# The blocks of a triangular solve turned by small products with an identity in place of full transposes

## The chip, the core and the metric

The kernel runs on one core of a Trainium2 chip. The metric is the device time of one execution in microseconds (us). Lower is better.

## The reference

Two layers of a hybrid network over 1,024 tokens of width 1,024 are computed in float32. What matters here is the mixer of the first layer: its linear recurrence of eight heads of 64 channels, run once forward and once backward in time, whose two outputs are added.

```python
def step(state, inp):
    r_t, w_t, k_t, v_t, kk_t, a_t = inp
    sk = jnp.einsum('bhij,bhj->bhi', state, kk_t)
    state = (state * w_t[:, :, None, :]
             - sk[..., :, None] * (kk_t * a_t)[:, :, None, :]
             + v_t[..., :, None] * k_t[:, :, None, :])
    y = jnp.einsum('bhij,bhj->bhi', state, r_t)
    return state, y
```

The other parts are the attention of three dilations, the Fourier mixer, the gated convolutions and the norms. The change does not touch them.

## The kernel before

The recurrence is not run token by token. The 1,024 tokens are cut into 16 chunks of CH = 64, two chunks to a pair, so NPAIR = 8 pairs for each direction g (0 forward, 1 backward). The eight heads are KU = 4 pairs of heads f, each with two heads hh. Within a chunk the steps are tied together by a unit lower triangular matrix of 64x64 (built from `xn`), one for each head and each chunk c. There are 16 such matrices for each pair of chunks, and each has to be inverted.

The inverse is built in five levels (LEVELS 2, 4, 8, 16, 32) by doubling: blocks of size b that are already inverted are joined to blocks of size 2b. A level i has four steps, with the engine that does each:

- `turn_u` on TensorE: the present inverse (`X1` at level 0, `T` after it) is transposed into bank 2 of PSUM. ScalarE copies the result to `U` (L1915).
- `level_x` on TensorE (L1749): products of the triangular matrix with the present inverse. VectorE puts the wanted blocks into `XL` by a predicated copy (L2079).
- `level_t` on TensorE (L1780): products of `U` with `XL`. VectorE copies them to `T` (L2087, L2089). At the last level `last_u` (L1792) takes this place, and ScalarE copies its result to `T` (L1921).

`T` and `X1` hold 128 partitions by 8 matrices by 64 columns. The two chunks of a pair lie in the two halves of the partitions (`side(c)`), and the two heads of a pair lie in the two halves of the output's partitions after the turn (`head(hh)`). Each group g has four banks of PSUM of its own: `bank(g, 0)` to `bank(g, 3)`. Bank 2 takes the transposes. Bank 3 takes the products of `values` (L1732), which ScalarE copies to `rz` (L1909, semaphore `mv_c`), and in other steps parts of `turn`, `scores`, `solve`, `step_open` and `last_u`.

The order on each engine is written out by hand, in a loop of half steps h. In each half step one direction (a) goes through the five levels of its inverse, while the other (b) uses its finished inverse (`solve` L1804, `carry` L1815, `step_open` L1829 and L1834, `step_close` L1846 and L1850) and prepares its next pair (`turn` L1689, `scores` L1708, `lower` L1720, `values` L1732). In the next half step the two change places. Sixteen half steps have levels, so `turn_u` runs 80 times. TensorE's order within a half step is:

```
turn_u 0, level_x 0, solve, level_t 0, carry,
turn_u 1, level_x 1, step_open 1, level_t 1, step_open 0, step_close 0,
turn_u 2, level_x 2, step_close 1, level_t 2, turn (parts 0 and 1),
turn_u 3, level_x 3, scores 0, level_t 3, scores 1,
turn_u 4, level_x 4, lower, values, last_u
```

ScalarE's order is: the copy of `turn_u` 0, those of `solve`, the copies of `turn_u` 1 and 2 with other work between them, `tokens` part 0, `turn_u` 3, `tokens` part 1, exponentials, `turn_u` 4, `values`, `last_u`. SyncE loads five or six factors of 256 KB in each half step.

Most matrix products here are 64x64 pieces: they use one quadrant of TensorE's array, given by the half of the partitions that they read and the half that they write. The trace calls this form 64*64. A product in this form appears in the trace as two weight loads and two matmuls, as 16 calls give x32 in its rows. A full transpose (form 128*128) appears as one of each.

Of the kernel before, what the change touches and what calls it, by code (L numbers as in the profile page):

```python
# [11 lines left out]
ACT = mybir.ActivationFunctionType  # L12
AX = mybir.AxisListType

P = 128
# [522 lines left out]
CH = 64  # L538
# [3 lines left out]
KU = WA // P  # L542
# [934 lines left out]
def recurrence(nc, z_d, vr_d, lw_d, aa_d, kk_d, consts, ysum, mix_out, bon_d, gate_d, yb_d, factors, small):  # L1477
# [5 lines left out]
    ident = consts["ident"]  # L1483
# [3 lines left out]
    with ExitStack() as ctx:  # L1487
        s = Scope(nc, ctx, "rw")

        def both(name, shape, dt=F32):  # L1490
            return [s.sb(f"{name}{g}", shape, dt) for g in range(2)]
# [15 lines left out]
        X1, _, T, U = (both(n, [P, UN, CH]) for n in ("X1", "align", "T", "U"))  # L1507
# [12 lines left out]
        pb = s.ps("pb", [P, 8, 512])  # L1520
        pw = pb[:, :, :].rearrange("p k (f n) -> p (k f) n", n=P)

        def sems(name):
            return [s.sem(f"{name}{g}") for g in range(2)]
# [3 lines left out]
        turned, tok_c, q_done, q_c, l_done, x1_c, mv_done, mv_c = (sems(n) for n in (  # L1528
            "turned", "tok_c", "q_done", "q_c", "l_done", "x1_c", "mv_done", "mv_c"))
        x_done, x_c, t_done, t_c, u_done, u_c, z_done, z_c, rg_done, rg_c = (sems(n) for n in (  # L1530
            "x_done", "x_c", "t_done", "t_c", "u_done", "u_c", "z_done", "z_c", "rg_done", "rg_c"))
# [8 lines left out]
        def side(c):  # L1540
            return slice((1 - c) * CH, (2 - c) * CH)
# [4 lines left out]
        def head(hh):  # L1546
            return slice(hh * HD, (hh + 1) * HD)
# [10 lines left out]
        def bank(g, k):  # L1558
            return pb[:, 4 * g + k, :]
# [18 lines left out]
        def pair(f, hh):  # L1578
            return 2 * f + hh
# [86 lines left out]
        def _(pe):  # L1666
            mm = nc.tensor.matmul
# [84 lines left out]
            def turn_u(g, m, i):  # L1752
                if not 0 <= m < NPAIR:
                    return
                if i == 0:
                    pe.wait_ge(x1_c[g], 2 * m + 2)
                    pe.wait_ge(q_c[g], 4 * m + 3)
                else:
                    pe.wait_ge(t_c[g], (NL - 1) * m + i)
                src = X1[g] if i == 0 else T[g]  # L1760
                for f in range(KU):
                    ins = nc.tensor.transpose(bank(g, 2)[:, f * P:(f + 1) * P], src[:, 2 * f:2 * f + 2, :].rearrange("p h n -> p (h n)"),
                                              ident[:, :])
                ins.then_inc(u_done[g], 1)

            def level_t(g, m, i):
# [87 lines left out]
            for h in range(-1, 2 * NPAIR + 1):  # L1854
                a, p, b, q = h % 2, h // 2, 1 - h % 2, (h - 1) // 2
                turn_u(a, p, 0)
                level_x(a, p, 0)
                solve(b, q)
                level_t(a, p, 0)
                carry(b, q)  # L1860
                turn_u(a, p, 1)
                level_x(a, p, 1)
                step_open(b, q, 1)
                level_t(a, p, 1)
                step_open(b, q, 0)
                step_close(b, q, 0)
                turn_u(a, p, 2)
                level_x(a, p, 2)
                step_close(b, q, 1)
                level_t(a, p, 2)  # L1870
                turn(b, q + 1, 0)
                turn(b, q + 1, 1)
                turn_u(a, p, 3)
                level_x(a, p, 3)
                scores(b, q + 1, 0)
                level_t(a, p, 3)
                scores(b, q + 1, 1)
                turn_u(a, p, 4)
                level_x(a, p, 4)
                lower(b, q + 1)  # L1880
                values(b, q + 1)
                last_u(a, p)

        @block.scalar
        def _(act):
            A = nc.scalar.activation
# [24 lines left out]
            def turn_u(g, m, i):  # L1911
                if not 0 <= m < NPAIR:
                    return
                act.wait_ge(u_done[g], (NL + 1) * m + i + 1)
                A(U[g].rearrange("p (c f) n -> p f c n", c=2), bank(g, 2).rearrange("p (f c n) -> p f c n", c=2, n=CH), ACT.Copy).then_inc(u_c[g], 1)  # L1915

            def last_u(g, m):
                if not 0 <= m < NPAIR:
# [58 lines left out]
            for h in range(-1, 2 * NPAIR + 1):  # L1977
                a, p, b, q = h % 2, h // 2, 1 - h % 2, (h - 1) // 2
                turn_u(a, p, 0)
                solved_z(b, q)  # L1980
                solved_w(b, q)
                turn_u(a, p, 1)
                f_rates(a, p + 1)
                turn_u(a, p, 2)
                out(b, q, 0)
                out(b, q, 1)
                tokens(b, q + 1, 0)
                turn_u(a, p, 3)
                tokens(b, q + 1, 1)
                f_exp_in(a, p + 1)  # L1990
                f_exp_before(a, p + 1)
                turn_u(a, p, 4)
                f_exp_out(a, p + 1)
                values(b, q + 1)
                last_u(a, p)
# [1893 lines left out]
```

## Time and profile before

| what | value |
|---|---|
| median of 3 runs | 2735.75 us |
| lowest and highest of them | 2735.1 and 2738.48 us |
| span of the profiled execution | 2735.4 us |
| its time outside the span | no record of its own; 2735.4 stands for it |
| mean granted clock of TensorE | 0.963 |
| stretch of the recurrence | about 643 to 1012 us |

The profile is of one execution. The span goes from its first to its last instruction. A row of the timeline shows when a group began and how long it lasted in all; instructions in a group overlap, so that the distance from one start to the next is what a group costs its engine. PEld is the loading of weights, PE the matmul, DVE VectorE, ACT ScalarE, POOL GpSimd, SP SyncE. "Issue" in brackets is idle time that no semaphore of the profile ends. The queue called q8 carries the program's own instructions.

### The profile page before, as it was taken

What the parts mean: (1) busy time and instruction counts of PE and PEld (TensorE: products, weight loads), DVE (VectorE), ACT (ScalarE), POOL (GpSimd) and SP (SyncE); (2) the same over time, 40 slices, a digit from 0 to 9 for tenths busy, and PEclk for the clock granted to TensorE, in tenths of its full rate; (3) what the DMA queues carried; (4) which work ended last, traced back from release to release, by engine and by line L of the source; (5) the groups of instructions that cost most, each with busy time, mean ns of one, the idle gap of its engine ahead of it and who ended that gap; (6) DMA issues with size and microseconds to landing.
All of it is one profiled execution on the core that took longest, in us unless ns stands there. A gap on an engine that the chain in (4) does not pass through costs nothing. (4 is left out here: it accounts for less than half of the span.)

```text
span 2735.4 us, 51474 instructions
## 1 busy us (share of the span) xinstructions
PE 2545.9 (93%) x21459; PEld 2056.0 (75%) x21459; DVE 1554.7 (57%) x2258; ACT 1158.6 (42%) x1818; POOL 906.6 (33%) x629
## 2 busy tenths in 40 slices
PE   5998989898999989789999999996988999999998
PEld 4776656566888877678888888775767888888887
DVE  7775622464666646655555564456565555556445
ACT  5211252464555533434444444453443434444434
POOL 2301121212222202247877720001324787772000
PEclk7999999998999989999999999998999999999999
DMA  7686534812222123222323265441222232326554
GB/s 241 216 279 218 174 124 168 255 25 75 77 73 73 50 88 132 77 78 85 93 70 93 82 235 187 167 144 72 85 77 80 82 93 70 92 86 237 188 176 146
DMA packets 295914, 346.27 MB, mean 127 GB/s; under 512 B 28383, under 2 KB 224212, under 8 KB 295684
## 3 DMA queue, kind: packets, MB, share of 16 engines
q1 hardware_dynamic: 286044, 336.64, 37.7%
q10 hardware_dynamic: 9640, 6.33, 0.8%
q8 instruction: 172, 2.82, 0.4%
q14 instruction: 58, 0.48, 0.1%
HBM read 271.58 MB, written 71.34 MB: 125 GB/s over the span
## 5 line engine op out<-in xcount | busy, mean ns | idle before, releaser
L3138 POOL TENSOR_TENSOR cg_u_lo<-cg_u_raw,cg_u_hi 128x512 fp32r<-128x512 f32 x210 | 314.5, 1506 | 148.1 <-ACT cg_u_hi L3024 148.1
L131 PE MATMUL cg_ps<-m_hi,cg_u_hi 128*128 128x512 f32 x844 | 331.5, 393 | 26.1 <-DVE cg_u_lo L3213 21.8
L133 PE MATMUL cg_ps<-m_hi,cg_u_lo 128*128 128x512 f32 x844 | 330.8, 392 | 0.0
L132 PE MATMUL cg_ps<-m_lo,cg_u_hi 128*128 128x512 f32 x808 | 316.3, 391 | 0.0
L3024 ACT ACTIVATE cg_u_hi<-cg_u_raw 128x512 fp32r<-128x512 f32 x216 | 132.1, 629 | 381.0 <-PE cg_ps L133 230.6
L131 PEld LDWEIGHTS cg_ps<-m_hi,cg_u_hi 128*128 128x128 f32 x844 | 160.0, 190 | 61.2 <-DVE cg_u_lo L3213 22.6
L133 PE MATMUL cg_ps<-over_y_tx,cg_u_lo 128*128 128x512 f32 x480 | 186.9, 389 | 0.0
L132 PE MATMUL cg_ps<-over_y_tx,cg_u_hi 128*128 128x512 f32 x480 | 186.9, 389 | 0.0
L131 PE MATMUL cg_ps<-over_y_tx,cg_u_hi 128*128 128x512 f32 x480 | 186.9, 389 | 0.0
L133 PEld LDWEIGHTS cg_ps<-m_hi,cg_u_lo 128*128 128x128 f32 x844 | 159.9, 189 | 33.5
L3190 DVE SCALAR_TENSOR_TENSOR cg_z<-cg_ps,top_conv_f,cg_z 128x1023 f32<-128x1023 f32 x88 | 112.9, 1283 | 115.7 <-ACT cg_z L3048 115.7
L132 PEld LDWEIGHTS cg_ps<-m_lo,cg_u_hi 128*128 128x128 f32 x808 | 152.8, 189 | 31.6
L3138 POOL TENSOR_TENSOR cg_u_lo<-cg_u_s,cg_u_hi 128x512 fp32r<-128x512 f32 x80 | 103.6, 1296 | 63.7 <-ACT cg_u_hi L3024 63.7
L3193 DVE SCALAR_TENSOR_TENSOR cg_z<-cg_ps,top_conv_f,cg_z 128x1023 f32<-128x1023 f32 x88 | 112.9, 1283 | 3.1
L131 PE MATMUL za_ps<-h_hi,za_w_hi 128*128 128x512 f32 x256 | 105.8, 413 | 7.4 <-POOL za_w_lo L1039 7.4
L3048 ACT ACTIVATE cg_z<-cg_ps,top_conv_f 128x1024 f32<-128x1024 f32 x88 | 98.2, 1116 | 21.0 <-DVE cg_ps L3250 11.6
L132 PEld LDWEIGHTS cg_ps<-over_y_tx,cg_u_hi 128*128 128x128 f32 x480 | 90.1, 188 | 18.7
L133 PEld LDWEIGHTS cg_ps<-over_y_tx,cg_u_lo 128*128 128x128 f32 x480 | 90.1, 188 | 18.7
L131 PEld LDWEIGHTS cg_ps<-over_y_tx,cg_u_hi 128*128 128x128 f32 x480 | 90.1, 188 | 18.7
L131 PE MATMUL cg_ps<-over_f_d_hi,cg_a_hi 128*128 128x512 f32 x248 | 97.0, 391 | 6.4 <-DVE cg_a_lo L3209 6.4
L132 PE MATMUL za_ps<-h_lo,za_w_hi 128*128 128x512 f32 x256 | 102.8, 402 | 0.0
L133 PE MATMUL za_ps<-h_hi,za_w_lo 128*128 128x512 f32 x256 | 102.4, 400 | 0.0
(497 smaller groups left out, 6216.2 us busy)
## 6 DMA issues: line engine op xcount, KB each, us to landing
cg_u_raw<-in_ffn_up SPq DMA_DIRECT2D x88, 512.0 KB, 5.1
cg_u_raw<-in_ffn_down SPq DMA_DIRECT2D x64, 512.0 KB, 4.8
qkv_mw<-in_ada_w SPq DMA_DIRECT2D x12, 2048.0 KB
over_f_d_raw<-in_ffn_down SPq DMA_DIRECT2D x48, 512.0 KB, 5.0
scr_act<-cg_z SPq DMA_DIRECT2D x44, 512.0 KB, 2.7
qkv_mw<-in_ada_w SPq DMA_DIRECT2D x8, 1024.0 KB, 11.7
next_w<-in_mix_in SPq DMA_DIRECT2D x16, 512.0 KB, 6.0
za_out<-in_ada_w SPq DMA_DIRECT2D x8, 1024.0 KB
```

The costliest lines, as they stand in the source:

```text
L131: nc.tensor.matmul(out, a_hi, b_hi, start=first, stop=False)
L132: nc.tensor.matmul(out, a_hi, b_lo, start=False, stop=False)
L133: return nc.tensor.matmul(out, a_lo, b_hi, start=False, stop=last)
L3024: A(u_hi[:, n % RING], source(g, i), ACT.Copy).then_inc(uhi_done, 1)
L3048: A(z[:, x, :], both(g, x), ACT.Copy, scale=conv_cols[:, 1, g + x * FT:g + x * FT + 1]).then_inc(mid_done, 1)
L3138: G.tensor_tensor(u_lo[:, n % RING], source(g, i), u_hi[:, n % RING].bitcast(F32), ALU.subtract).then_inc(ulo_done, 1)
L3190: V.scalar_tensor_tensor(z[:, x, 1:S], both(g, x)[:, 0:S - 1], conv_cols[:, 0, c:c + 1], z[:, x, 1:S], ALU.mult, ALU.add).then_inc(left_do ...
L3193: V.scalar_tensor_tensor(z[:, x, 0:S - 1], both(g, x)[:, 1:S], conv_cols[:, 2, c:c + 1], z[:, x, 0:S - 1], ALU.mult, ALU.add).then_inc(con ...
```

## The change

At each of the 80 places the four full transposes of 128x128 are replaced by 16 products of 64x64: the piece of `X1` or `T` is the stationary operand, and the piece of the identity on the same partitions is the moving operand, so that the result is the piece transposed. The products for chunk c = 0 go to bank 3 and those for c = 1 to bank 2, in columns 0 to 255 of each. ScalarE's copy reads the two banks instead of one and writes `U` in its order in memory. As bank 3 is now written, the first `turn_u` of a half step waits for the copy of `values` out of it (`mv_c`), and for the fourth instead of the third masked copy of `scores` (`q_c`).

```diff
@@ turn_u on TensorE
                 if i == 0:
                     pe.wait_ge(x1_c[g], 2 * m + 2)
-                    pe.wait_ge(q_c[g], 4 * m + 3)
+                    pe.wait_ge(q_c[g], 4 * m + 4)
+                    pe.wait_ge(mv_c[g], m + 1)
                 else:
                     pe.wait_ge(t_c[g], (NL - 1) * m + i)
                 src = X1[g] if i == 0 else T[g]
                 for f in range(KU):
-                    ins = nc.tensor.transpose(bank(g, 2)[:, f * P:(f + 1) * P], src[:, 2 * f:2 * f + 2, :].rearrange("p h n -> p (h n)"),
-                                              ident[:, :])
+                    for hh in range(2):
+                        for c in range(2):
+                            ins = mm(bank(g, 3 - c)[head(hh), f * CH:(f + 1) * CH], src[side(c), pair(f, hh), :], ident[side(c), side(c)],
+                                     start=True, stop=True)
                 ins.then_inc(u_done[g], 1)
@@ turn_u on ScalarE
-                A(U[g].rearrange("p (c f) n -> p f c n", c=2), bank(g, 2).rearrange("p (f c n) -> p f c n", c=2, n=CH), ACT.Copy).then_inc(u_c[g], 1)
+                A(U[g].rearrange("p (c f) n -> p c (f n)", c=2), pb[:, 4 * g + 2:4 * g + 4, 0:KU * CH], ACT.Copy).then_inc(u_c[g], 1)
```

## Rows read from the trace of the kernel before

**Rows 1.** The page: span, busy times of TensorE, the instruction queue.
```profile
span 2735.4 us, 51474 instructions
...
PE 2545.9 (93%) x21459; PEld 2056.0 (75%) x21459; DVE 1554.7 (57%) x2258; ACT 1158.6 (42%) x1818; POOL 906.6 (33%) x629
...
q8 instruction: 172, 2.82, 0.4%
```

**Rows 2.** Busy times by window, inside the recurrence (from:to, length, engines, clock, DMA).
```profile
660.00:990.00 330.00, 320.21 (x9618) 289.72 (x9618) 196.07 (x408) 180.55 (x361) 69.19 (x55) 0.99 0.24 72
```

**Rows 3.** Groups by line and form, the recurrence: the transposes' matmuls.
```profile
L1762 PE MATMUL rw_pb<-top_ident,rw_T 128*128 128x128 f32 x256 | 41.8, 287 | 2.4 <-DVE rw_T L2089 1.6 <-DVE rw_T L2087 0.8
...
L1762 PE MATMUL rw_pb<-top_ident,rw_X 128*128 128x128 f32 x64 | 10.5, 287 | 0.0
```

**Rows 4.** Timeline of weight loads: four starts of the solve.
```profile
674.85 0.14 PEld L1804 LDWEIGHTS rw_pb<-rw_rz,rw_T 64*64 64x64 f32 x2
...
872.08 0.31 PEld L1804 LDWEIGHTS rw_pb<-rw_rz,rw_T 64*64 64x64 f32 x6
...
893.37 0.31 PEld L1804 LDWEIGHTS rw_pb<-rw_rz,rw_T 64*64 64x64 f32 x6
...
981.61 0.20 PEld L1804 LDWEIGHTS rw_pb<-rw_rz,rw_T 64*64 64x64 f32 x4
```

**Rows 5.** Timeline of weight loads between two gaps, 721 to 726 us.
```profile
721.00 0.21 PEld L1780 LDWEIGHTS rw_pb<-rw_XL,rw_U 64*64 64x64 f32 x8 [0.38 <-issue]
721.12 0.86 PEld L1815 LDWEIGHTS rw_pb<-rw_xn,rw_zt 64*64 64x64 f32 x32
722.16 0.42 PEld L1762 LDWEIGHTS rw_pb<-top_ident,rw_T 128*128 128x128 f32 x4 [0.18 <-DVE rw_T L2087]
722.75 0.56 PEld L1749 LDWEIGHTS rw_pb<-rw_T,rw_xn 64*64 64x64 f32 x32 [0.17 <-issue]
723.35 0.55 PEld L1829 LDWEIGHTS rw_pb<-rw_wv,rw_xn 128*64 128x64 f32 x16
723.81 0.55 PEld L1834 LDWEIGHTS rw_pb<-rw_xn,rw_wv 128*64 128x64 f32 x16
724.43 0.43 PEld L1780 LDWEIGHTS rw_pb<-rw_XL,rw_U 64*64 64x64 f32 x20
725.78 0.31 PEld L1780 LDWEIGHTS rw_pb<-rw_XL,rw_U 64*64 64x64 f32 x12 [0.92 <-issue]
```

**Rows 6.** DMA queues, windows 723.3:723.4, 834.2:834.3 and 837.5:837.7 us (packets, MB, share).
```profile
q8 instruction: 1, 0.02, 72.2%
...
q8 instruction: 1, 0.02, 55.5%
...
q8 instruction: 1, 0.02, 29.2%
```

**Rows 7.** Timeline of weight loads, 804 to 818 us.
```profile
804.31 0.56 PEld L1720 LDWEIGHTS rw_pb<-rw_st 64*64 64x64 f32 x32
804.78 1.03 PEld L1732 LDWEIGHTS rw_pb<-rw_wv,rw_xn 64*64 64x64 f32 x32
...
806.34 0.42 PEld L1762 LDWEIGHTS rw_pb<-top_ident,rw_X 128*128 128x128 f32 x4
...
807.39 1.51 PEld L1804 LDWEIGHTS rw_pb<-rw_rz,rw_T 64*64 64x64 f32 x28
...
815.05 0.54 PEld L1846 LDWEIGHTS rw_pb<-rw_es,rw_rg 64*64 64x64 f32 x16
815.51 0.55 PEld L1850 LDWEIGHTS rw_pb<-rw_rg,rw_es 64*64 64x64 f32 x16
816.13 0.43 PEld L1762 LDWEIGHTS rw_pb<-top_ident,rw_T 128*128 128x128 f32 x4
816.72 0.56 PEld L1749 LDWEIGHTS rw_pb<-rw_T,rw_xn 64*64 64x64 f32 x32 [0.16 <-issue]
817.19 0.55 PEld L1846 LDWEIGHTS rw_pb<-rw_es,rw_rg 64*64 64x64 f32 x16
```

**Rows 8.** Timeline of ScalarE: the copy of the values.
```profile
806.00 0.60 ACT L1909 ACTIVATE rw_rz<-rw_pb 128x512 f32<-128x512 f32 x1 [0.93 <-PE rw_pb L1732]
```

## The prediction

> **What bounds the kernel now.** I read the page first. TensorE is busy 93% of the span, and the queue that carries instructions has moved 172 packets [rows 1]. Then I looked at the recurrence by window: over 330 us TensorE is busy for 320 us at a clock of 0.99, while VectorE and ScalarE are busy for 196 and 181 us [rows 2]. So inside this stretch the order of TensorE is nearly closed, and what it costs from one start to the next sets the time. The recurrence stands between barriers, so its end moves the kernel's end one for one. The matmuls' mean of 287 ns [rows 3] can't be used for this: four of them begin within 0.43 us, because they overlap. The distances between starts have to be read from the timeline.
>
> A half step shows itself as the distance between two starts of the solve. From 674.85 to 981.61 us there are 14 of them, 21.91 us each. A half step in which nothing is late takes 893.37 - 872.08 = 21.29 us [rows 4]. So 0.62 us of each half step is lost to something that comes and goes. What it is matters most here.
>
> The rows between 721 and 726 us show it. Weight loads stop in the middle of a group at a gap called "issue", begin again at 721.00, stop again in the middle of a group, and begin again at 725.78, with 0.92 us idle before it. No semaphore ends either gap. Counted, there are 8 + 32 + 4 + 32 + 16 + 16 + 20 = 128 loads from the first gap to the second [rows 5]. Each load has its matmul, so 256 instructions. The page gives the same number from the other side: 42,918 loads and matmuls in 172 packets are 250 to a packet, and instructions that only wait, which these counts leave out, fill up the rest [rows 1]. A packet is thus 256 of TensorE's instructions, and a gap stands where one packet is used up and the next is not there. The packet for 725.78 is seen in the queue at 723.3 [rows 6], 2.4 us before its first use and 2.3 us after TensorE had begun the packet ahead of it. I read this as a supply one packet deep: the next packet is asked for when the present one is begun, and it can be used only after one to two us of queueing and 2.4 us more. TensorE can't go faster than one packet per 4.78 us there. Where the queue is less loaded it is quicker: two packets follow each other in 837.6 - 834.2 = about 3.4 us [rows 6], with no gap near them.
>
> **The change on TensorE's own account, for one half step.** A group of four transposes costs 816.72 - 816.13 = 0.59 us from start to start. The 16 products that replace it have the form of `lower` (L1720): 64 columns, all four quadrants, two banks. That group costs 804.78 - 804.31 = 0.47 us [rows 7]. So each of the five blocks gives back 0.12, in sum -0.60.
>
> Changing the form of the array costs time of its own. L1850 before the transposes costs 816.13 - 815.51 = 0.62, the like group L1846 before another of the same form 0.46 [rows 7], so a change of form costs 0.16. The turns 0, 1 and 2 come after groups of form 64*64 and lose this change on entry: -0.48. Turn 3 comes after the full transposes of `turn`. It enters without a change now and will need one: +0.16. Turn 4 comes after `scores`, which has yet another form, and changes either way: 0. The Trainium skill (TensorEngine Tiling (Array Packing), Key Properties) says that changing the tiling mode drains the engine; the trace agrees, with 0.16 for it. Sum so far: -0.92 us.
>
> Against that stand two waits. Turn 0 must wait for the copy of the values out of bank 3. That copy begins at 806.00 and lasts 0.60 [rows 8]. The turn starts at 806.34 today, and without its entry it could start at 806.18. With the wait it starts at about 806.67 (an estimate: 0.07 for the semaphore), so +0.49. Behind it on TensorE are `level_x` 0 and the solve, both late by as much; ScalarE's copy of turn 0 and VectorE's copy of `XL` are late next, with the solve (1.5 us [rows 7]) as cover before `level_t` 0 wants them. If the values' copy came earlier, the price would be nothing. The second wait is at turns 3 and 4. There ScalarE's copies for `tokens` and VectorE's masked copies for `scores` run end to end, and I take the 0.24 that these two blocks give back as lost, so +0.24; the bound below is 0. The copy of `U` moves the same 512 columns and is taken as unchanged. In sum -0.19 (bounds -0.92 and 0), and a half step with all packets on time goes from 21.29 to 21.1 us.
>
> **The change for the supply of instructions.** A group of transposes is 8 instructions (x4 loads, x4 matmuls). The 16 products are x32 and x32, as in L1720 [rows 7], so 64. That is 56 more at each place, 280 in a half step. Now 9,618 loads and as many matmuls in 330 us [rows 2] are 1,277 for each 21.91 us, 5.0 packets. With the change it is 1,557, or 6.1 packets. The need was one packet per 21.29 / 5.0 = 4.26 us. It becomes one per 21.1 / 6.1 = 3.46 us, close to the quickest supply seen (3.4) and far under the slow one (4.78). No packet of the instruction queue is added anywhere else.
>
> How long TensorE waits for each is not in the trace of before, so I bound it. Now the wait is 0.62 / 5.0 = 0.12 us for each packet. It can't be less with a shorter need: floor 0.12. It can't grow by more than the need shrinks (0.80): ceiling 0.92. Between them I need the mean supply. It must be under 4.26, or most packets would be late now and half steps of 21.29 would hardly occur; it is over 3.4. I take 3.75, as gaps are not rare. Then the need is short by 0.29 on average, and the mean wait is at least 0.29, and more because both vary, by about as much as it is 0.12 today in spite of 0.5 of slack: 0.42. For a half step: 6.1 x 0.42 = 2.56, so 21.1 + 2.56 = 23.66 against 21.91, which is +1.75. One of the sixteen half steps, the first, waits for other things, so 15 x 1.75 = +26. From 2735.4 that gives 2761 us; the median of the runs is 0.35 above the span, which I leave aside.
>
> The Trainium skill (Runtime: NRT & Kernel Launch, Instruction fetch mechanics) states the page of 256 instructions and the fetch of the next while the present one runs, but calls the cost of a boundary "mostly hidden" and gives TensorE a store of several pages. By that page the supply term would be about nothing. The rows of 721 to 726 us speak against it.
>
> **The rivals.**
> *The supply stays hidden.* Condition: more packets are in store than I read, and the gaps have another cause. Then only TensorE's account counts: 16 x -0.19 = -3, to 2732 us, which is no measurable change (within 0.2%, 5.5 us, is about what a measurement of this kernel can't tell from none). For it: 0.62 us for each half step is all that is lost now. Against it: the distance of exactly 256 instructions. The skill's page named above leads to this result. Chance 0.14.
> *The gain arrives in full.* This is the other side: the supply is hidden and the wait for bank 3 is covered as well, since ScalarE gets the values' copy out sooner or the solve takes up the delay. 16 x -0.92 = -15, to 2721 us. It decides if the mean wait for a packet stays at 0.12 and turn 0 starts before 806.4. Chance 0.08.
> *The supply is slow throughout.* If every fetch meets the load seen at 721 us (4.78), a half step is 6.1 x 4.78 = 29 us and the kernel is over 2835; at the ceiling of 0.92 per packet it is 21.1 + 5.6 = 26.7, +4.8, to 2807. SyncE's loads are the same number in a longer half step, which speaks against it. Chance 0.06 for above 2785.
> *The forecast*, limited by the supply in part: 0.72.
>
> **How the numbers follow.** The likeliest case spans waits of 0.29 to 0.65 per packet: 21.1 + 1.8 = 22.9 gives +15 and 2750; 21.1 + 4.0 = 25.1 gives +48 and 2783. Its predicted time is 2761. The whole range, 2732 to 2785, takes in the hidden supply down to its centre. Slower by over 0.2%: 0.72 + 0.06 = 0.78. Within 0.2%: 0.14. Faster: 0.08.
>
> **What would show each step.** After the change a group of turn products and the `level_x` after it should start 0.47 apart. L1850 before turn 2 should cost 0.46 and not 0.62. Turn 0 should start when the copy of the values has ended, and q8 should show about 17 to 18 packets more (4,480 / 256). The decisive sign is that gaps called "issue" in the middle of groups, 128 loads apart, are several in each half step, and that the solve starts 23 to 24 us apart. If those gaps are as rare as now, the supply step is wrong and the time lies at 2721 to 2735. If the turn's group costs well over 0.47, TensorE's account is wrong.

## The result and the profile after

The changed kernel takes 2792.73 us (median of 4 runs, 2783.73 to 2794.28) against 2737.11 for the kernel before (2735.1 to 2743.28). The ratio is 1.019, with an interval of 1.0169 to 1.0211. It was forecast as slower, at 2761, in a range of 2732 to 2785: the direction was right, the loss is 55.6 us instead of 26, and the time lies 8 us above the range.

The page of the changed kernel:

```profile
span 2790.6 us, 55954 instructions
...
PE 2557.2 (92%) x23699; PEld 2073.8 (74%) x23699; DVE 1552.0 (56%) x2258; ACT 1159.7 (42%) x1818; POOL 907.0 (33%) x629
...
q8 instruction: 189, 3.10, 0.5%
```

Loads and matmuls have grown by 2,240 each, and the instruction queue carries 17 packets more than in [rows 1]. The span has grown by 55.2 us; busy PE has grown by only 11. Two starts of the solve, on the timeline of weight loads, answer to [rows 4]:

```profile
677.15 0.14 PEld L1807 LDWEIGHTS rw_pb<-rw_rz,rw_T 64*64 64x64 f32 x2
...
1032.21 0.31 PEld L1807 LDWEIGHTS rw_pb<-rw_rz,rw_T 64*64 64x64 f32 x6
```

Fourteen half steps lie between them, as between the first and last row of [rows 4], and they take 25.36 us each instead of 21.91. That is 14 x 3.45 = 48 us of the 55. Where a half step has lost it can be seen from 800 to 813 us, again on the timeline of weight loads:

```profile
804.54 0.32 PEld L1783 LDWEIGHTS rw_pb<-rw_XL,rw_U 64*64 64x64 f32 x14 [0.77 <-issue]
804.74 0.89 PEld L1818 LDWEIGHTS rw_pb<-rw_xn,rw_zt 64*64 64x64 f32 x32
805.80 0.56 PEld L1765 LDWEIGHTS rw_pb<-top_ident,rw_T 64*64 64x64 f32 x32 [0.17 <-DVE rw_T L2090]
806.26 0.56 PEld L1749 LDWEIGHTS rw_pb<-rw_T,rw_xn 64*64 64x64 f32 x32
806.87 0.55 PEld L1832 LDWEIGHTS rw_pb<-rw_wv,rw_xn 128*64 128x64 f32 x16
807.33 0.20 PEld L1837 LDWEIGHTS rw_pb<-rw_xn,rw_wv 128*64 128x64 f32 x2
808.83 0.54 PEld L1837 LDWEIGHTS rw_pb<-rw_xn,rw_wv 128*64 128x64 f32 x14 [1.31 <-issue]
```

From the gap before 804.54 to the gap before 808.83 there are 14 + 32 + 32 + 32 + 16 + 2 = 128 loads, as in [rows 5], and again the gaps stand in the middle of a group. The 128 loads now begin within 2.8 us, up to the load group at 807.33, and then TensorE stands still until 808.83. The DMA queues of the changed kernel in two short windows (801.9:802 and 806.5:806.6) show when the packets for these two places passed, 2.6 and 2.3 us ahead of their first use:

```profile
q8 instruction: 1, 0.02, 72.0%
...
q8 instruction: 1, 0.02, 66.8%
```

The place of the gaps can be counted over the whole stretch. In these fourteen half steps there are 42 places where two loads of one group begin more than 0.4 us apart. Counted over all of TensorE's records in the trace (loads, matmuls and waits, in order of their starts), all 42 stand at the same place of a block of 256, give or take one record. The same count gives 303 of 303 in the traces of all kernels of this text but the one with added waits.

One half step, the last of the fourteen, takes 29.22 us; the other thirteen take 25.06 on average (22.93 and 21.83 in the kernel before). Most of its excess is one gap:

```profile
1013.55 0.25 PEld L1853 LDWEIGHTS rw_pb<-rw_rg,rw_es 64*64 64x64 f32 x5
1017.50 0.40 PEld L1853 LDWEIGHTS rw_pb<-rw_rg,rw_es 64*64 64x64 f32 x6 [3.70 <-issue]
```

TensorE began the packet ahead of this one at 1010.7, and the packet passed the queue at 1014.9. In between, q1, the queue of the data loads, kept the DMA engines busy for 94% of the time (DMA view, 1010.7 to 1014.8); SyncE had issued three loads for the next stage from 1009.3 on.

```profile
q1 hardware_dynamic: 737, 1.48, 94.1%
```

A long gap also has a second price. Within or soon after gaps of 2.05, 1.54, 2.09 and 3.70 us the granted clock of TensorE stands at its lower level (1.2 GHz) for 3.4, 3.4, 3.4 and 6.8 us. The first and the last of these stretches, by window (clock in the third place from the end):

```profile
685.20:688.60 3.40, 3.40 (x77) 3.10 (x73) 0.43 (x1) 0.00 (x0) 1.30 (x2) 0.51 0.47 135
1016.30:1023.10 6.80, 5.60 (x72) 5.20 (x75) 0.85 (x2) 1.58 (x3) 0.00 (x0) 0.50 0.45 164
```

The fourteen half steps of the kernel before have no such stretch. The 17 us at the lower level cost at most half of that, 8.5 of the 48 us (an estimate).

TensorE's own account can be read where no packet is late. These rows of the same timeline answer to [rows 7]:

```profile
938.64 0.54 PEld L1849 LDWEIGHTS rw_pb<-rw_es,rw_rg 64*64 64x64 f32 x16
939.11 0.43 PEld L1853 LDWEIGHTS rw_pb<-rw_rg,rw_es 64*64 64x64 f32 x12
939.40 0.13 PEld L1765 LDWEIGHTS rw_pb<-top_ident,rw_T 64*64 64x64 f32 x1
...
944.63 0.56 PEld L1765 LDWEIGHTS rw_pb<-top_ident,rw_T 64*64 64x64 f32 x32 [0.17 <-issue]
945.09 0.56 PEld L1749 LDWEIGHTS rw_pb<-rw_T,rw_xn 64*64 64x64 f32 x32
...
952.16 0.59 PEld L1765 LDWEIGHTS rw_pb<-top_ident,rw_X 64*64 64x64 f32 x32 [0.16 <-issue]
```

A turn costs 0.46 (944.63 to 945.09). L1853 costs 0.29 before turn 2 (939.11 to 939.40), even less than a group before its like, since the first products of the turn slip in among its last ones. Turn 0 starts at 952.16. The copy that it waits for is this one, on the timeline of ScalarE, which answers to [rows 8]:

```profile
951.45 0.60 ACT L1912 ACTIVATE rw_rz<-rw_pb 128x512 f32<-128x512 f32 x1 [0.77 <-PE rw_pb L1732]
```

It ends at 952.05, and the turn starts 0.11 later.

### The profile page after: what moved, and what is told of

Same layout as the page of the kernel before. It is cut to its first block and busy times, and to the rows that moved or that the text cites. A ratio compares the mean times of both kernels' runs of the same rounds, so it can differ in the third digit from the quotient of the medians.

```text
span 2790.6 us, 55954 instructions
## 1 busy us (share of the span) xinstructions
PE 2557.2 (92%) x23699; PEld 2073.8 (74%) x23699; DVE 1552.0 (56%) x2258; ACT 1159.7 (42%) x1818; POOL 907.0 (33%) x629
```

## The experiments

The theory is the one of the prediction: TensorE's instructions arrive in packets of 256, one packet ahead, and the change asks for more packets in less time. The rivals are the form and the banks of the new products, and the new wait at turn 0. In each run "before" is the kernel before on the same chip, and runs of different chips are best compared by their ratios.

### Half of the products, each twice as wide

```diff
-                for f in range(KU):
+                for f in range(KU // 2):
                     for hh in range(2):
                         for c in range(2):
-                            ins = mm(bank(g, 3 - c)[head(hh), f * CH:(f + 1) * CH], src[side(c), pair(f, hh), :], ident[side(c), side(c)],
+                            ins = mm(bank(g, 3 - c)[head(hh), f * P:(f + 1) * P], src[side(c), pair(f, hh), :], ident[side(c), :],
```

> The changed kernel with 8 products at each turn instead of 16, each with a moving operand of 128 columns instead of 64 (the identity's two halves). TensorE's columns stay the same, the instructions of a turn fall from 64 to 32. Half of U is not what the reference needs. Supply of instructions: a half step needs 5.5 packets instead of 6.1; the wait for each falls from 0.69 us to about 0.35, TensorE's own account stays near 21.2 us, so a half step falls from 25.4 to about 23.2 and the time from 2792 to about 2760 (2750 to 2772). Rival, the products themselves or their two banks are what costs (form of the array, PSUM, the copy's new pattern): nothing changes, 2787 to 2797.

Measured: 2758.45 us, ratio 1.0073 (1.0054 to 1.0093). The solve's starts on its timeline of weight loads, 14 half steps apart, give 23.28 us:

```profile
679.67 0.14 PEld L1807 LDWEIGHTS rw_pb<-rw_rz,rw_T 64*64 64x64 f32 x2
...
1005.54 0.14 PEld L1807 LDWEIGHTS rw_pb<-rw_rz,rw_T 64*64 64x64 f32 x2
```

With the form, the banks, the wait and the copy of the change all in place, 32 instructions fewer at each turn give back 34 of the 56 us. The rival of form and banks falls, and the size comes out as expected.

### Turn 0 with full transposes again

```diff
                 if i == 0:
                     pe.wait_ge(x1_c[g], 2 * m + 2)
-                    pe.wait_ge(q_c[g], 4 * m + 4)
-                    pe.wait_ge(mv_c[g], m + 1)
+                    pe.wait_ge(q_c[g], 4 * m + 3)
...
+                if i in (1, 2, 3, 4):
...
+                else:
+                    for f in range(KU):
+                        ins = nc.tensor.transpose(bank(g, 2)[:, f * P:(f + 1) * P], src[:, 2 * f:2 * f + 2, :].rearrange("p h n -> p (h n)"),
+                                                  ident[:, :])
```

> The changed kernel with the full transposes back at turn 0 alone, and so without the wait for the copy of the values. Supply: 56 instructions fewer in a half step (0.22 packets, 0.9 us) and 0.2 us on TensorE's own account: 16 to 18 us less, about 2775. Rival, the wait for bank 3 at turn 0 is the cause: nearly all of the loss goes, about 2740.

Measured: 2771.05 us, ratio 1.0121 (1.0104 to 1.0138): 22 us less than the change by the medians and 19 by the ratios, a little more than expected, and far from the 2740 of the rival.

### The kernel before with the new waits alone

```diff
-                    pe.wait_ge(q_c[g], 4 * m + 3)
+                    pe.wait_ge(q_c[g], 4 * m + 4)
+                    pe.wait_ge(mv_c[g], m + 1)
```

> The kernel before with only the two waits of the change at turn 0 (the fourth masked copy of scores, and the copy of the values). Supply: about 0.34 us for each of 16 half steps on TensorE's own account, +5 us, 2742 or less since a late packet can arrive during the wait. Rival, the wait is the cause: above 2765.

Measured: 2739.97 us, ratio 1.0013 (1.0003 to 1.0023), a loss of 1 to 6 us. The wait is real and small. A half step grows by 0.14 us, less than the 0.37 by which TensorE alone takes longer (21.66 against 21.29), and the waiting for each packet falls from 0.12 to 0.08. That a late packet comes in during the new wait would explain it; no run shows it by itself.

### Instructions that only wait

```diff
+            def pad(m, n):
+                for _ in range(n):
+                    pe.wait_ge(eye_set, 1)
...
                     for f in range(KU):
+                        pad(m, 8)
                         ins = nc.tensor.transpose(bank(g, k)[:, f * P:(f + 1) * P], src[:, f, :], ident[:, :])
```

`scores` got 4 and `solve` 5 of them ahead of each product.

> The kernel before with 272 waits more in each half step on a semaphore that has long been reached, ahead of the transposes of turn and the products of scores and solve, where the array is the slowest to take instructions. Their computation is nothing; the instructions are about as many as the change adds (280). Supply: gaps 128 loads apart are no longer the pattern, but gaps that no semaphore ends appear, the instruction queue carries about 17 packets more and the time rises by 35 to 60 us, to 2772 to 2797, if each wait costs TensorE's sequencer little. Rival, instructions cost nothing but their issue: no more than +5 us, unless each wait takes so long that the groups that hold them grow, which the distances of their starts would show.

Measured: 2903.09 us, ratio 1.0605 (1.0585 to 1.0625). This run does not decide anything about the packets. Its own condition failed: the waits are not cheap. On its timeline of weight loads, transposes of `turn` that had started about 0.11 us apart before now start 0.44 apart with eight waits written ahead of each:

```profile
936.24 0.14 PEld L1694 LDWEIGHTS rw_pb<-top_ident,att_over_h_q 128*128 128x128 f32 x1 [0.30 <-issue]
936.68 0.18 PEld L1694 LDWEIGHTS rw_pb<-top_ident,att_over_h_q 128*128 128x128 f32 x1 [0.30 <-issue]
```

The trace also shows only 2,048 instructions more than before (53,522 against 51,474, 128 in a half step) and 8 packets more, not 17. Of the eight waits written ahead of a transpose, four stand in the trace as instructions, each 0.106 us after the one before. The time can't be laid to the waits alone either: from 700 to 1000 us the mean granted clock is 0.83, against 0.99 in [rows 2]. A test that adds instructions has to add such as cost the engine next to nothing. The next one comes close.

### The same products in twice the instructions, in the kernel before

```diff
@@ solve (carry is split in the same way)
                         for c in range(2):
-                            ins = mm(bank(g, 2 + hh)[side(c), f * P:(f + 1) * P], T[g][side(c), pair(f, hh), :], rz[g][side(c), hh * KU + f, :],
-                                     start=True, stop=True)
+                            for n in range(0, P, CH):
+                                ins = mm(bank(g, 2 + hh)[side(c), f * P + n:f * P + n + CH], T[g][side(c), pair(f, hh), :],
+                                         rz[g][side(c), hh * KU + f, n:n + CH], start=True, stop=True)
```

> The kernel before, transposes and all, with each product of solve and carry (128 moving columns) made as two of 64 columns: the same columns through the array, the same results, 128 instructions more in a half step (5.5 packets instead of 5.0). Supply: like the run with half of the turn's products, 23.2 us for a half step, +20 us, about 2757 (2748 to 2768), with solve and carry no longer by themselves than now where no packet is late. Rival, the number of instructions does not matter and the turn's products cost: 2735 to 2741.

Measured: 2772.0 us, ratio 1.0126 (1.0111 to 1.0141), 15 us above the expected value and 4 above its range, with nothing of the change in it. The turns are the four transposes in this run, and a gap stands after 127 or 128 loads all the same, on its timeline of weight loads:

```profile
706.76 0.60 PEld L1817 LDWEIGHTS rw_pb<-rw_xn,rw_zt 64*64 64x64 f32 x28 [0.20 <-issue]
707.43 0.42 PEld L1762 LDWEIGHTS rw_pb<-top_ident,rw_T 128*128 128x128 f32 x4
708.02 0.56 PEld L1749 LDWEIGHTS rw_pb<-rw_T,rw_xn 64*64 64x64 f32 x32 [0.17 <-issue]
708.62 0.55 PEld L1831 LDWEIGHTS rw_pb<-rw_wv,rw_xn 128*64 128x64 f32 x16
709.08 0.55 PEld L1836 LDWEIGHTS rw_pb<-rw_xn,rw_wv 128*64 128x64 f32 x16
709.70 0.55 PEld L1780 LDWEIGHTS rw_pb<-rw_XL,rw_U 64*64 64x64 f32 x31
710.69 0.13 PEld L1780 LDWEIGHTS rw_pb<-rw_XL,rw_U 64*64 64x64 f32 x1 [0.43 <-issue]
```

28 + 4 + 32 + 16 + 16 + 31 = 127 loads in 3.93 us. Part of the time is TensorE's own: with the split, the typical distances of the groups sum to 21.75 us in a half step instead of 21.29, which is 7 us in sixteen half steps. The rest of the 33 us over the kernel before, some 26, is not.

### Fewer loads beside the packets

```diff
+            def part_load(dst, src, sem):
+                sp.dma_start(dst[0:8, :, :], src.rearrange("f p t -> p f t")[0:8]).then_inc(sem, 16)
...
-                    load(kx[g], z_d[KU:2 * KU, :, tokens_of(g, m)], f_loaded[g])
+                    part_load(kx[g], z_d[KU:2 * KU, :, tokens_of(g, m)], f_loaded[g])
```

The loads of `rx` and `kk` were cut in the same way, first in the changed kernel.

> The changed kernel with three of SyncE's factor loads of each half step (k, r and kk) cut to 8 of 128 partitions, so that the factors are old for the rest. TensorE's work and instructions are the same. If a packet of instructions comes late because it queues behind these loads, the wait for each falls from 0.69 to about 0.4 us and the time by about 25 us, to 2767 (2755 to 2775). If the delay of a packet has nothing to do with the loads, or if the packets are not the cause, it stays at 2787 to 2797.

Measured: 2781.91 us, ratio to before 1.0163 (1.0147 to 1.018): 7 us less than the change by the ratios and 11 by the medians, not 25. Then the same in the kernel before:

> The kernel before with the same three loads cut. Queueing behind loads: most of the 0.6 us that is lost in a half step now is given back, 5 to 9 us in all, 2728 to 2732. No queueing: 2735 to 2740. It is also the base that shows what the loads themselves are worth.

Measured: 2730.7 us, ratio 0.9975 (0.9962 to 0.9988), 8 us less. So in the kernel before queueing behind these three loads delays the packets, but it is a small part of what a packet takes. In the changed kernel the profiles don't show even that: the distances of over 0.3 us from load to load at the ends of packets sum to 54.8 us in the fourteen half steps with whole loads and to 55.3 with small ones. What fell there is the time at the lower clock, from 17 to 3.4 us, as gaps of 2 us became rarer. The expectation for the changed kernel was wrong by more than half.

### The change at fewer turns

With the 16 products at turns 1 and 2 alone (`if i in (1, 2)` around them, transposes elsewhere, the old wait at turn 0):

> The change at turns 1 and 2 alone (those with the largest gain on TensorE's own account, 0.3 us each, and no new wait), the transposes elsewhere. 112 instructions more in a half step, 5.4 packets. Supply: TensorE alone 20.7 us, with waits of 0.35 us for each packet 22.6, against 21.9 now: +10 us, about 2747 (2740 to 2754). If packets cost nothing: -9 us, 2728.

Measured: 2760.29 us, ratio 1.0081 (1.0066 to 1.0096). TensorE's own part came out as forecast, at 20.77 us, and the half step still grew to 23.67, past the 22.6 that was expected; the time is 6 us above the range.

With the products at turn 2 alone:

> The change at turn 2 alone, where it meets no new wait and both neighbours have its form: 56 instructions more in a half step, 0.3 us less on TensorE's own account. By the pace of 4.2 us a packet: 5.36 x 4.2 = 22.5 us against 21.9, +9 us, about 2747 (2741 to 2752). By the prediction's slack of 0.5 us under each packet: 2733 to 2739, no measurable change.

Measured: 2744.81 us, ratio 1.0011 (0.9996 to 1.0026). The profiled half step is 22.62 us, as the pace of 4.2 gives (22.31 without the last of the fourteen, which takes 26.56), but the timed loss is smaller, and its interval holds 1. This run doesn't decide between the two.

### More and fewer instructions still

The changed kernel with `solve` and `carry` split:

> The changed kernel with solve and carry split as in the run of the kernel before with split products: 128 instructions more in a half step, 6.6 packets. In all runs so far a packet of 256 instructions took TensorE 4.1 to 4.3 us in the recurrence, whatever it held. If that is the supply's own pace, a half step becomes 6.6 x 4.2 = 27.9 us against 25.4, and the time about 2830 (2818 to 2842). If instead each packet costs a fixed wait of 0.67 us on top of TensorE's own time, it is 21.7 + 6.6 x 0.67 = 26.1 and 2804.

Measured: 2815.96 us, ratio 1.0277 (1.0243 to 1.0312), in the middle between the two values and 2 us under the range of the first. The solve's starts, on its timeline of weight loads:

```profile
679.06 0.19 PEld L1808 LDWEIGHTS rw_pb<-rw_rz,rw_T 64*64 64x64 f32 x3
...
1055.68 0.25 PEld L1808 LDWEIGHTS rw_pb<-rw_rz,rw_T 64*64 64x64 f32 x5
```

That is 26.90 us for 6.71 packets, 4.01 each. Neither reading was right as it stood: the pace is not one fixed number, and the wait for a packet is not fixed either.

The kernel before with 96 instructions fewer in a half step:

```diff
@@ step_open, the y side (step_close and values in the same way)
-                for f in range(KU):
+                for f in range(KU // 2):
                     for hh in range(2):
                         w, x = wv[g][:, c, hh * KU + f, :], xn[g][:, hh, 2 * f + c, :]
-                        mm(y_out[head(hh), f * CH:(f + 1) * CH], w, x[:, CH:2 * CH], start=(f == 0), stop=False, skip_group_check=True)
+                        mm(y_out[head(hh), f * P:(f + 1) * P], w, x[:, CH:3 * CH], start=(f == 0), stop=False, skip_group_check=True)
```

> The kernel before with half of the products of values and of the y side of step_open and step_close, each of double width: the same columns through the array, 96 instructions fewer in a half step (4.8 packets), transposes as before; half of these products' results are not what the reference needs. By the pace of 4.2 us the supply then needs 20 us and TensorE 21.3: the half step goes from 21.9 to about 21.4, 5 to 9 us less, 2729 to 2733. If the kernel before does not stand at the supply's limit: 2735 to 2740.

Measured: 2729.13 us, ratio 0.9968 (0.9951 to 0.9986). On its timeline of weight loads, 14 half steps again:

```profile
675.52 0.20 PEld L1804 LDWEIGHTS rw_pb<-rw_rz,rw_T 64*64 64x64 f32 x4
...
975.09 0.20 PEld L1804 LDWEIGHTS rw_pb<-rw_rz,rw_T 64*64 64x64 f32 x4
```

21.40 us: of the 0.51 us that a half step has lost, 0.17 is TensorE's own (21.12 against 21.29) and 0.34 is waiting for packets. The kernel before stands at the edge of the supply.

### All runs side by side

All values are for one half step, from the same 14 in each trace. "Alone" is the sum of the typical (median) distance from each group's start to the next: what TensorE takes when no packet is late. Packets are those that q8 shows in the stretch.

| kernel | packets | alone, us | half step, us | us per packet | wait per packet |
|---|---|---|---|---|---|
| before, fewer instructions | 4.71 | 21.12 | 21.40 | 4.54 | 0.06 |
| before | 5.14 | 21.29 | 21.91 | 4.26 | 0.12 |
| before, small loads | 5.07 | 21.29 | 21.69 | 4.28 | 0.08 |
| before, new waits alone | 5.14 | 21.66 | 22.05 | 4.29 | 0.08 |
| products at turn 2 | 5.29 | 21.02 | 22.62 | 4.28 | 0.30 |
| products at turns 1 and 2 | 5.50 | 20.77 | 23.67 | 4.30 | 0.53 |
| change, half of the products | 5.57 | 21.05 | 23.28 | 4.18 | 0.40 |
| before, split | 5.57 | 21.75 | 23.88 | 4.29 | 0.38 |
| change, turn 0 transposed | 6.00 | 20.95 | 24.47 | 4.08 | 0.59 |
| change | 6.14 | 21.26 | 25.36 | 4.13 | 0.67 |
| change, small loads | 6.14 | 21.28 | 24.95 | 4.06 | 0.60 |
| change, split | 6.71 | 22.45 | 26.90 | 4.01 | 0.66 |

The run with added waits is left out, since its waits and its clock are mixed into its half step. The last column holds what the lower clock costs as well, at most 0.10 us in the change and 0.15 in its split version (estimates from 17 and 27 us at that level).

The time that TensorE takes alone moves little down this table, and not with the half step. The half step follows the packets. From the kernel before on, a packet takes 4.0 to 4.3 us, whichever instructions are in it.

## Why the prediction went wrong in size

**TensorE's own account: right.** 0.47 for a turn was forecast and is 0.46. The change of form is gone at turn 2. The copy of the values holds turn 0 back as forecast (the turn starts 0.11 us after the copy's end, taken as 0.07). The whole was to go from 21.29 to 21.1 and is 21.26. It is right as a sum, while its parts moved more than forecast and offset each other (medians, start to start): the group before turn 2 gives back 0.32 (0.62 to 0.30), twice the forecast, but `level_x` 2 and `level_t` 3 take 0.16 and 0.19 more. The run with the new waits alone shows that the wait for bank 3 is worth 1 to 6 us of the 56.

**The count: right.** 17 to 18 packets more were forecast, and there are 17. A half step was to need 6.1 and needs 6.14.

**One packet ahead: shown.** Gaps in the middle of groups, at the same place of every block of 256 instructions, are the pattern of the changed kernel, as the prediction named it. In 84 of its 86 intervals from one packet's first use to the next, exactly one packet passes q8. And more instructions for the same columns cost 33 us in the kernel before, some 26 of them waiting, where nothing else of the change was present. The products' form and banks are no cause of it: the run with half as many, twice as wide, keeps both.

**The wait for each packet: the term that was mis-sized.** The prediction came to 0.42 us of waiting per packet. The traces show (25.36 - 21.26) / 6.14 = 0.67. The floor and the ceiling that it set (0.12 and 0.92) do hold it; the step between them failed, in three parts.

The first is the mean supply, taken as 3.75 us. Once the packets' places are known, it can be read for all of them. In the changed kernel a packet passes q8 on average 1.41 us after TensorE has begun the one ahead of it (from 0.42 to 4.13), and where a gap in the middle of a group waits for it, it is used 2.5 us later: 3.9 in all. In the kernel before it is 1.23 + 2.5 = 3.7. So 3.75 was right for the kernel before and 0.15 short for the change. That it was so near is partly luck: it is a value between 4.26 and 3.4, and the 3.4 [rows 6] is the distance of two passages with no gap near them, not an interval that the supply had ended.

The second is the need. Its mean was forecast as 3.46 and is 3.42 (the interval from packet to packet less the gap at its end). But TensorE uses packets up in 2.3 to over 5 us, by what they hold. Of the 44 that it used up in under 3.2 us, 35 were followed by a gap of over 0.3; of the 26 that lasted over 3.8 us, 4 were. A supply of exactly 3.75 us would make TensorE wait 0.50 on average against these needs, and one of 3.9 would make it wait 0.61 (estimates worked out from the trace). The prediction took the shortfall of the means, 0.29, and 0.13 for all unevenness.

The third is the clock, which the prediction left out: the lower level after long gaps adds at most 0.10. With 0.67 in the prediction's own sum a half step is 21.1 + 6.1 x 0.67 = 25.2 us, against 25.36 measured.

The second reading, a fixed pace of 4.2 us, was formed from the runs above it in this text and fell too. It gave 2830 for the split version, which took 2816. The pace goes from 4.26 to 4.01 as the need gets denser. It is a mixture of packets that TensorE waited for and of packets that lasted long enough to cover the next.

**The rivals.** "The supply stays hidden" and "the gain arrives in full" did not happen. "The supply is slow throughout" had the right mechanism, with prices (2807 to over 2835) that were too high, and got 0.06. Of the two ways to go wrong about a supply read from a trace, too fast and too slow, the chances had nearly left out the second, although the only interval in the rows that the supply itself had ended was the slow one, 4.78 us [rows 5].

The page of the Trainium skill (Runtime: NRT & Kernel Launch, Instruction fetch mechanics) is confirmed in its packet of 256 instructions and in the fetch of one while the other runs. That this is "mostly hidden" does not hold here: it is most of the difference between 2737 and 2793 us.

**What stays open.** Why a packet takes about 4 us from the moment TensorE begins the one ahead of it. Its last 2.2 to 3.2 us, from its passage in the queue to its first use after a gap in the middle of a group, are much the same in all traces. The rest, 1.1 to 1.5 us on average, depends only slightly on SyncE's three cut loads. It can grow beside others, as the 4.1 us to 1014.9 show, where the loads of the next stage held the DMA engines; those loads and the ones that were left in each half step were not varied. Of the 55 us in the span, 3 us lie outside the recurrence (its last weight-load group starts 52.2 us later), within what the runs of one kernel differ by. No run that makes the whole computation beat the kernel before.

## What to carry to other kernels

Before many small products take the place of a few large ones, count instructions as well as columns: a dense stretch of TensorE has a limit in instructions per microsecond, here some 256 in 4 us, and its sign is idle time called "issue" in the middle of a group, at equal counts of instructions. A stretch that shows a few such gaps already stands at the limit, and most of what it is given more is paid for: here 8 packets more cost 33 us, and 17 cost 56. To size such a supply, take the intervals that the supply itself ended, not the shortest that was ever seen, and set them against what each packet needs, not against the mean need.

## What the runs showed of the hardware

A wait on a semaphore that had long been reached is not free on TensorE: four such instructions ahead of each transpose (eight were written) moved its start from 0.11 to 0.44 us after the one before. And a half step whose products move the same columns runs 0.5 us faster when the number of its instructions falls by 96 (21.91 to 21.40), although the busy share of TensorE, 97% in [rows 2], had left no room to be seen.
